# A two-block transformer kernel: second norm's first rows and scale beside the projection, weight totals asked later, every second dilation-16 row pair taken out by ScalarE

## The reference, cut to what matters

```python
def reference(...):                                  # S=2048 rows, D=1024, batch 1
    x = first_block(x, ...)                          # norm, w_in, gating / conv / window attention, w_out, layer norm
    return second_block(x, norm_pre_g_2, w_in_2, conv_w_2, w_out_2, norm_post_g_2)

def second_block(x, g, w_in, conv_w, w_out, g_post):
    h = rmsnorm(x, g)
    q, k, v, g_attn, c_h, c_b, c_c, g_conv = split(h @ w_in)      # 4 x 768 and 4 x 256 columns
    q, k = rope(q), rope(k)                                       # 12 heads of 64
    for window, dilation in ((128, 1), (512, 4), (2048, 16)):
        o_i, lse_i = dilated_window_attn(q, k, v, window, dilation)
    o = sum(softmax(lse) * o_i) * silu(g_attn)
    conv_out = c_b * causal_depthwise_conv(c_c * c_h, conv_w) * silu(g_conv)
    return x + rmsnorm(concat(o, conv_out) @ w_out, g_post)
```

## Time and profile before

| | us |
|---|---|
| runs | 2291.33, 2297.74, 2300.50 |
| median | 2297.74 |
| profiled execution, its time | 2291.84 |
| its span, first to last instruction | 2289.7 |
| PE busy in the span | 2082.4 |
| DVE busy | 1394.7 |
| ACT, POOL busy | 923.1, 906.7 |

### The profile page before, as it was taken

One profiled execution on the slowest core, in us unless ns is written; L12 is line 12 of the kernel. 1 busy time (PEld: TensorE's weight loads), 2 busy tenths in 40 slices (PEclk: granted clock), 3 DMA queues, 4 the chain that ended last, 5 costly groups with the idle time before them and its releaser, 6 DMA issues.

```text
span 2289.7 us, 43310 instructions
## 1 busy us (share of the span) xinstructions
PE 2082.4 (91%) x16228; PEld 1525.7 (67%) x16228; DVE 1394.7 (61%) x3507; ACT 923.1 (40%) x1981; POOL 906.7 (40%) x1004
## 2 busy tenths in 40 slices
PE   5999999997898999499999999999988888887998
PEld 3545868886787888488644444656877766666786
DVE  7614949765897444773376772213179999994422
ACT  3323333222796000232233431211179999883111
POOL 4311333363422999332111211211132888983222
PEclk9999999998899999799999999999999999997999
DMA  5441321346633232442344431321156787674552
GB/s 180 134 110 57 108 80 44 92 142 201 154 80 107 79 109 98 156 135 66 115 118 137 117 116 49 117 73 55 49 123 161 195 197 185 169 220 135 161 172 90
DMA packets 285536, 279.95 MB, mean 122 GB/s; under 512 B 39712, under 2 KB 237216, under 8 KB 285072
## 3 DMA queue, kind: packets, MB, share of 16 engines
q1 hardware_dynamic: 281280, 271.08, 41.1%
q0 software_dynamic: 1680, 5.51, 0.6%
q10 hardware_dynamic: 2368, 0.60, 0.1%
HBM read 171.22 MB, written 93.31 MB: 116 GB/s over the span
## 4 chain that ended last, share of the span: by engine, by line
PE 27%; DVE 16%; issue 4%; ACT 2%; POOL 2%; DMA 2%; SPq 1%; DVEq 0%; ACTq 0%; POOLq 0%
PE bank L172 19%; PE bank L2507 7%; DVE s2m L2357 6%; DVE p2l L2363 4%; DMA qr<-qf 1%; DVE qf L1801 1%; SPq L1830 1%; ACT s2sh L1781 1%; DVE qr L1799 1%; DVE s2sl L1804 1%; DVE qf L1798 1%; DVE ob L2369 1%; PE bank L2302 1%; POOL qs L2399 0%; ACT p2r L2336 0%
## 5 line engine op out<-in xcount | busy, mean ns | idle before, releaser
L172 PE MATMUL bank<-xh,w2l 128*128 128x512 f16 x640 | 244.7, 382 | 0.0
L172 PE MATMUL bank<-xh,w2h 128*128 128x512 f16 x640 | 244.5, 382 | 0.0
L172 PE MATMUL bank<-xl,w2h 128*128 128x512 f16 x640 | 244.5, 382 | 0.0
L172 PE MATMUL bank<-w1h,xh 128*128 128x256 f16 x768 | 212.6, 277 | 3.0 <-DVE s1st L918 3.0
L172 PE MATMUL bank<-w2h,xh 128*128 128x256 f16 x768 | 211.3, 275 | 2.0 <-issue 2.0
L2302 PE MATMUL bank<-ident,p2r 128*128 128x128 f32 x900 | 165.9, 297 | 51.9 <-DVE p2l L2363 45.7
L172 PE MATMUL bank<-w1l,xh 128*128 128x256 f16 x768 | 212.5, 277 | 0.0
L172 PE MATMUL bank<-w1h,xl 128*128 128x256 f16 x768 | 212.4, 277 | 0.0
L172 PE MATMUL bank<-w2h,xl 128*128 128x256 f16 x768 | 211.2, 275 | 0.0
L172 PE MATMUL bank<-w2l,xh 128*128 128x256 f16 x768 | 211.2, 275 | 0.0
L2302 PEld LDWEIGHTS bank<-ident,p2r 128*128 128x128 f32 x900 | 97.4, 145 | 108.5 <-DVE p2l L2363 105.7
(11 more groups left out here) (345 smaller groups left out, 5643.1 us busy)
## 6 DMA issues: line engine op xcount, KB each, us to landing
scr_part<-ob SPq DMA_DIRECT2D x48, 264.0 KB, 3.2
cm<-scr_part SPq DMA_DIRECT2D x48, 264.0 KB, 4.7
v<-scr_v SPq DMA_DIRECT2D x192, 65.0 KB, 2.6
w2r<-in_w_in SPq DMA_DIRECT2D x12, 1024.0 KB, 6.4
qr<-qf SPq DMA_DIRECT2D x192, 64.0 KB, 2.0
ax<-in_x SPq DMA_DIRECT2D x16, 512.0 KB, 5.3
xr<-in_x SPq DMA_DIRECT2D x16, 512.0 KB, 4.4
bx<-scr_x SPq DMA_DIRECT2D x16, 512.0 KB, 6.2
```

The source lines that it names most:

```text
L172: ins = nc.tensor.matmul(dst, x, y, start=k == 0 and m == 0, stop=k == n - 1 and m == 2)
```

## The change

Four things change. (1) `project_stage` also loads the second norm's first four row tiles and first weight chunk, into buffers of their own on the right side of SBUF, and works out the gain's size, the statistics and the scaled rows; `norm_stage("b")` starts with `turn(0)` and takes them from `ahead`. (2) In both norm stages `total 2` and `total 3` stand behind groups that used to follow them; in the gate stage the total stands behind tile 3 instead of tile 1 and `act_scale` before tile 5. (3) For d = 16, too, ACT copies out every second pair. (4) The 17000-column pad that kept stage b's buffers clear of the project stage's is gone, and `take_over` now comes first on every engine that has it.

```diff
 class Weights:
+        def raw_of(self, n):
+            return self.first[0] if n == 0 and self.first is not None else self.raw[n % 2]
 norm_stage:
-        if late:
-            sb(f"{tag}pad", [128, 17000], scope=scope)
-        work = [("wide",), ("load", 0)]
+        work = [("load", 0)] if late else [("wide",), ("load", 0)]
...
             if g == 1:
-                work += [("load", 2), ("total", 2)]
+                work.append(("load", 2))
+            if g == 2:
+                work.append(("total", 2))
...
-        work += [("consts",), ("load", 3), ("total", 3)]
-        work += [("group", 2, 0), ("scaled", 3)] + [("group", 2, g) for g in range(1, 4)]
+        work += [("consts",), ("load", 3)]
+        work += [("group", 2, 0), ("total", 3), ("group", 2, 1), ("scaled", 3), ("group", 2, 2), ("group", 2, 3)]
...
-                    pe.wait_ge(*d_sc.at(4 * g + 4))
+                    pe.wait_ge(*(ahead["scaled"] if late and g == 0 else d_sc.at(4 * (g - off) + 4)))
...
         def sp_program():
-            sp_fetch(0)
             take_over(sp)
-            wts.sp_load(0)
+            if not late:
+                sp_fetch(0)
+                wts.sp_load(0)
             wts.sp_load(1)
 project_stage:
+        def sp_ahead(n):
+            if n == 6:
+                nc.sync.dma_start(raw2[:], w2...[:, :, cols2:cols2 + 256]).then_inc(*w_in.up(16))
+            if 8 <= n < 12:
+                t = n - 8
+                sp.wait_ge(*x_out[t].at(16))
+                nc.sync.dma_start(rows2[t][:], x1[128 * t:128 * t + 128, :]).then_inc(*n_in[t].up(16))
+        def dve_ahead(n):
+            # n == 5: most, its square, own (4 small instructions); n == 8: whole; n == 11: whole, fitted
+            if 10 <= n < 14:
+                t = n - 10
+                dve.wait_ge(*n_in[t].at(16))
+                # two bn_stats of rows2[t], one bn_aggr
+            elif n == 14:
+                # three small instructions on rs2
+            elif n == 15:
+                dve.wait_ge(*g_nx.at(1))
+                for t in range(4):
+                    nc.vector.tensor_scalar(rows2[t][:], rows2[t][:], rs2[:, t:t + 1], None, ALU.mult).then_inc(*d_nx.up())
+        def pool_ahead(n):
+            # n == 10: three small instructions on own and whole; n == 14: the power of rs2
...
+                if n == 7:
+                    # PE: ones x own, one matmul of one column
...
                 if n + 2 < NT:
                     dve_residual(n + 2)
+                dve_ahead(n)
...
                 nc.gpsimd.tensor_tensor(rs[:, k:k + 1], rs[:, k:k + 1], power[:, 0:1], ALU.pow).then_inc(*g_pw.up())
+                pool_ahead(n)
 gate_stage:
-                if m % 8 == 1 and x["n"] in total_bank:
+                if m % 8 == 3 and x["n"] in total_bank:
                     wts.pe_total(first + x["n"] + 1, *total_bank[x["n"]])
...
-                if m % 8 == 4 and first + m // 8 + 1 < len(wts.chunks):
+                if m % 8 == 5 and first + m // 8 + 1 < len(wts.chunks):
                     wts.act_scale(first + m // 8 + 1)
 dilated_stage:
-                    on_act = x["d"] < 16 and x["g"] % 4 == 2
+                    on_act = x["g"] % 4 == 2
```

More of the change, by code:

```diff
@@ L175, in two_block_program, with __init__ @@
     class Weights:
-        def __init__(self, tag, scope, w, chunks, block):
+        def __init__(self, tag, scope, w, chunks, block, first=None):
             self.w = w.rearrange("(t p) n -> p t n", p=128)
@@ L215, in sp_load @@
                 return
-            if n > 1:
+            if n > (1 if self.first is None else 2):
                 sp.wait_ge(*self.ready[n - 2])
@@ L268, in act_scale @@
             act.wait_ge(*self.scaled[n])
-            nc.scalar.activation(self.raw[n % 2][:], self.raw[n % 2][:], ACT.Identity, scale=self.size[:, n, 3:4]).then_inc(*self.a_w.up())
+            nc.scalar.activation(self.raw_of(n)[:], self.raw_of(n)[:], ACT.Identity, scale=self.size[:, n, 3:4]).then_inc(*self.a_w.up())
         def pool_split(self, n):
@@ L297, in natural, with norm_stage @@
         return dst[256 * i:256 * i + 256, c:c + 256].rearrange("(u p) c -> p u c", p=128)
-    def norm_stage(tag, scope, src, gain, shift, gain_ready, x_ready, late, xh, xl, keep, wts, outs, heads, ones):
+    def norm_stage(tag, scope, src, gain, shift, gain_ready, ahead, late, xh, xl, keep, wts, outs, heads, ones):
         begin()
@@ L365, in norm_stage @@
             if item[0] == "wide":
[L366 removed]
+                wide_bank = bk.take(d_wd.at(3))
             elif item[0] == "total":
@@ L425, in dve_scale @@
             dve.wait_ge(*d_st.now())
-            dve.wait_ge(*g_pw.at(g + 1))
+            dve.wait_ge(*g_pw.at(g + 1 - off))
             for t in range(4):
@@ L599, in dve_program @@
         def dve_program():
-            if not keep:
-                dve_most()
-                dve_widest()
+            take_over(dve)
+            if not late:
+                dve_scale(0)
                 dve_widened()
[L604 to L607, removed]
             for item in work:
@@ L655, in pool_program @@
         def pool_program():
+            take_over(pool)
             if ones:
@@ L658, in pool_program @@
                     nc.gpsimd.memset(o[:, :, :, 64:66], 1.0).then_inc(*g_one.up())
-            if not keep:
+            if not late:
+                pool_power(0)
                 pool_widest()
[L661 to L664, removed]
             for item in work:
@@ new lines, in pool_ahead @@
+        def pool_ahead(n):
+            if n == 10:
+                pool.wait_ge(*d_wd.at(5))
+                nc.gpsimd.tensor_tensor(own, whole, power[:, 0:1], ALU.pow).then_inc(*g_wd.up())
+                pool.wait_ge(*g_wd.now())
+                nc.gpsimd.tensor_tensor(whole, whole, own, ALU.mult).then_inc(*g_wd.up())
+                pool.wait_ge(*g_wd.now())
+                nc.gpsimd.tensor_scalar(own, own, HTOP, None, ALU.mult).then_inc(*g_wd.up())
+            elif n == 14:
+                pool.wait_ge(*d_sx.at(15))
+                nc.gpsimd.tensor_tensor(rs2[:], rs2[:], power[:, 0:4], ALU.pow).then_inc(*g_nx.up())
@@ L1557, in pe_program @@
                     pe_turn(n + 1)
+                if n == 7:
+                    pe.wait_ge(*ONES)
+                    pe.wait_ge(*wide_bank[1])
+                    pe.wait_ge(*d_wd.at(4))
+                    nc.tensor.matmul(wide_bank[0][:, 0:1], ones_[:], own, start=True, stop=True).then_inc(*p_wd.up())
                 yh, yl = yt[n % 3]
@@ L1681, in project_stage @@
         pe_program()
-        return [(x_out[t], x_out[t].base + 16) for t in range(4)]
+        return dict(rows=rows2, scaled=d_nx.at(4), widened=d_gs.at(1), fitted=d_gs.at(2)), (raw2, w_in.at(16))
     def rope_stage(scope, wts, first, xh, xl):
@@ L1867, in gate_stage @@
                     tiles.append(x)
-                    if len(tiles) % 8 == 2 and first + n + 1 < len(wts.chunks):
+                    if len(tiles) % 8 == 4 and first + n + 1 < len(wts.chunks):
                         total_bank[n] = bk.take(wts.total[first + n + 1])
```

89 lines of the change are left out of this document (65 added, 24 removed).

## The result

The changed kernel takes 2256.83 us (median of four runs, 2252.40 to 2259.37) against 2296.85 for the kernel before (four runs): a ratio of 0.9826, with a 95% interval of 0.9800 to 0.9851. Forecast were 2261 us and 2252 to 2275. The profiled execution took 2252.40 us with a span of 2250.5, 39.2 less than the span before.

The account below looks back on a forecast made before the run. PE was busy 2082 of 2290 us, so time is won where it stands still or another engine, like DVE in the dilated stage, sets its pace. Terms 21.9 + 7.8 + 5.4 = 35.1 us gave 2261 us, range 2252 to 2275.

Parts of the forecast that it names:

- totals: Norm and gate stages: PE's five waits for ACT's sums vanish, 15.2 us idle plus 6.7 lost clock, 21.9 us.
- row pairs: Dilation 16: 24 copies go from DVE to ACT, 16 of them worth 0.34 us each, 5.4 us; last two stretches nothing.
- handover: Projection to second norm: first dense product at 947.5 instead of 955.32, 7.8 us gained; bounds 9.8 and 4.1.
- Rival 1: Norm and gate stages: the clock falls come up elsewhere, 6.7 us back, 2268 us; chance 0.13.
- rival 5: Norm and gate stages: PE's waits only move, to a bank or a scale, 11 us back, 2272 us; chance 0.09.
- the lower bound: Projection to second norm: gain of only 4.1 us, with the last store landing in 6.3 us.
- the prediction's own signs: Wrong if rests late for `group(0, 3)`, last store over 2 us later after PE's last product, or ACT awaits PE before copies.
- The store's delay: End of projection: last store issued 1.95 us later, from POOL's lateness (1.2) and DVE's scalings beside POOL's passes (0.75).
- rival 3: Projection to second norm: less gain, from a slow store landing or scalings behind POOL, 2265 us; chance 0.10.
- The landing of the last store: Projection's end: with row loads gone, 2.6 us like the stretch's median store, plus 0.1 for the semaphore; bound 6.3.
- rival 2: Dilation 16: ACT sets the pace, so the moved copies bring nothing, 5.4 us back, 2266 us; chance 0.09.
- rival 4: Dilation 16: ACT's copy waits for PE's product of its pair; 2316 us at 2.09 us each; chance 0.04.

## Why the prediction was right, point by point

The sum came out close (39.2 us in the traces, 40.0 by time, against 35.1), but not each term: totals and row pairs gave 1.4 and 1.1 us more than forecast, the handover 3.7 less, and 5.3 us came from stretches that were not in the sum. That the misses of the three terms nearly cancel, and that the rest did not carry the time further off, is luck. The totals, the largest term, carry the forecast.

**Totals: right, in mechanism and size.** 23.3 us in the trace and 25 (21 to 29) by time, against 21.9. The split into 15.2 idle and 6.7 clock is borne out by the run with idle products: 6.4 us for the clock alone. Rival 1 (the falls come up elsewhere) and rival 5 (the waits only move) did not come true here, and PE shows no wait for the rests of `group(0, 3)`.

**Handover: right in sign, too big; the sum's terms were off in three places.** It gave 5.4 in the gap less 1.3 in the projection, 4.1 against 7.8: the lower bound. By the prediction's own signs this part was wrong: the last store came 3.5 us later relative to PE's last product, where more than 2 was to mean wrong; SP was past `take_over` 3.76 us behind the store, not under 3; and ACT's first sum began 13.8 us behind that product, not 10.5. (1) The store's delay, 1.95 forecast, was 3.54. I had let DVE take the four scalings in 2.74 us and 0.75 us of the passes' disturbance reach the store. They took 6.99. That was rival 3's mechanism. The Trainium skill's rule (SBUF — State Buffer, "SBUF: two separate sides"), by which whoever comes second stands still for the whole other instruction, agrees with the trace: DVE loses 4.25 us while POOL's two passes run 2.39 and 2.71. ACT in the same place takes 4.28 us for the four without a gap and leaves POOL's passes at 2.40; no run has them on ACT without POOL beside it. (2) The landing of the last store, 2.7 with the semaphore, was 3.76, and about as long with the scalings elsewhere (ACT's sum 3.9 to 4.0 us behind the store in all three). The median of the other stores was the wrong row for it; why this one takes longer without the row loads beside it, no run shows. (3) The projection is 1.3 us longer, where the sum had nothing. I costed the engines' time for PE's one-column product in block 7 and not the bank it holds; that this wait of 1.3 us is the cause is likely, but not shown. From ACT's sum to the first product it was 15.7, not 16.2. The gap adds up: 1.6 us from (1), 1.3 from (2) as seen by ACT's sum (4.0 against 2.7), less 0.5, is the 2.4 by which 5.4 falls short of 7.8.

**Row pairs: right per copy, wrong in one stretch.** 0.33 us a copy and 3.83 us for four units, as forecast. That POOL's 40.7 busy of 43 us would leave nothing in the last two stretches was wrong in this trace: half of a copy's worth came through, 1.3 us, though other kernels with the same copies show less or none. I read the 0.95 as an engine that leads most of the time, not all of it; no run tests that. The 3.84 us did not hold for whole stretches (4.0 to 4.4), which were 4.2 to 4.6 before. ACT did not set the pace (rival 2), nor wait for PE (rival 4): with all copies on ACT the stage is still 2.7 us faster.

**The rest, 5.3 us, was in nobody's sum.** 3.9 lie between conv and projection. The stretch from the start of ACT's last four convolution taps to the projection's first product takes 326.9 and 327.3 us in two traces of the changed kernel, and 328.8 to 333.0 in the other twelve kernels, the kernel before (330.6) among them, though the instructions there are the same in all. PE's waits there are for DMAs (`my`, 11 to 15 us in sum) and for DVE. Between the kernel before and the changed one the difference is not in idle time: PE is busy for 279.4 us of it instead of 284.2, at a granted clock of 0.95 instead of 0.93, so the same products ran less long at the lower clock. Over all traces clock and waits both vary, and neither alone orders them. Whether it is chance or hangs on the build, two traces can't say. It explains why the store's 3.5 us, plain in the gap, did not show in the times. What a part is worth is better read between events around it than from the end.

## What to carry to other kernels

Where PE asks for a small result as soon as it could be there, ask one independent group later: it removed the wait and the half-clock stretch behind it, 1.7 us for each of four waits under 4.4 us. It pays only if the one who makes the result is late because of the order; if its own chain is the slow one, the wait turns up at the next question, as in the rope stage. When work is moved beside another stage, check not only busy time but what each moved instruction shares. The port shared with POOL cost 3.5 us here, and putting the scalings on idle ACT won them back in the gap; a bank in a ring may have cost another, which is not shown.

## What was unexpected

VectorE is not slowed by POOL at all times. In the kernel with the scalings on ACT, inside one of POOL's passes, `xr<-bank,xr` (one input from PSUM, one from SBUF) took 0.67 us as ever, and statistics 0.69:

```profile
904.71 2.40 POOL L1714 TENSOR_TENSOR xr<-xr,bcpb 128x1024 f32<-128x1024 f32 x1
905.49 0.69 DVE L1687 BATCH_NORM_STATS2 stP<-xr 128x6 f32<-128x512 f32 x1
906.10 0.67 DVE L1685 TENSOR_TENSOR xr<-bank,xr 128x512 f32<-128x512 f32 x1
```

But a 4-column addition of two SBUF operands took 2.38 us behind a POOL pass, here in the kernel with the scalings last, where that pass ran from 905.73 for 2.40 us:

```profile
905.76 2.38 DVE L1589 TENSOR_TENSOR rsN<-rsN,mvN 128x4 f32<-128x4 f32 x1
```

So its size does not decide whether an instruction stands behind POOL. The same page and section of the Trainium skill says that a DVE instruction with two SBUF inputs, or in a two-port mode, competes with POOL for the pair, and the trace agrees for the two inputs. The four scalings read only one SBUF tile of rows each and waited all the same, while the statistics, with one SBUF input too, did not; a mode is not visible in these rows, so that half of the rule is not tested here.
